# Fourier heads of a hybrid diffusion step: their map product moves into the last recurrent scan, their channel products beside the last recurrent norm, second half first

## The reference, cut to what matters

```python
o_h = o_f + jnp.flip(o_b, 1)
o_h = (_rms(o_h, hg_norm_w) * jax.nn.silu(hg.astype(F32).reshape(B, L, HG_HEADS, HG_DV)))
o_h = o_h.reshape(B, L, HG_WIDTH).astype(x.dtype)

xf = pft.astype(F32).reshape(B, L, FT_GROUPS, FT_CH)
mixed = jnp.real(jnp.fft.fft2(xf, axes=(1, 3), norm='ortho'))
o_ft = jnp.einsum('blgc,gce->blge', mixed, w_ft.astype(F32)).reshape(B, L, FT_WIDTH).astype(x.dtype)

mix = jnp.concatenate([o_attn, o_h, o_ft], axis=-1)
x = x + gate1 * jnp.einsum('blm,md->bld', mix, w_out)
```

## Time and profile before

| | us |
|---|---|
| median of 3 executions | 1788.07 |
| lowest, highest | 1786.11, 1788.44 |
| the profiled execution: its own time | 1787.74 |
| the profiled execution: span of the trace | 1785.9 |
| PE busy in the span | 1590.6 (89%) |
| DVE, ACT, POOL busy | 618.6, 387.3, 316.5 |
| mean granted TensorE clock | 0.944 of full speed |

### The profile page before, as it was taken

How to read it: one execution, slowest core, us unless ns; L and a number is a source line. 1 busy time by engine, 2 the same in 40 slices (tenths; PEclk the granted TensorE clock), 3 DMA queues, 4 the chain that set the end, 5 groups by cost and what they waited for, 6 DMA issues and landing times.

```text
span 1785.9 us, 24904 instructions
## 1 busy us (share of the span) xinstructions
PE 1590.6 (89%) x10358; PEld 1158.8 (65%) x10358; DVE 618.6 (35%) x1214; ACT 387.3 (22%) x718; POOL 316.5 (18%) x305
## 2 busy tenths in 40 slices
PE   6999989777898899999969998987879859999995
PEld 5556567556555788888755655766655458888883
DVE  1241246666115112222154312756631331221224
ACT  2231246222004100000142312632210210000002
POOL 4000159322000100000010001953300010000002
PEclk9999999878899899999979999998899969999997
DMA  9922100413022999999962211022400079999985
GB/s 267 327 54 69 50 27 2 143 52 94 0 71 107 340 363 366 365 363 359 339 237 47 67 52 50 2 72 73 120 1 1 1 272 329 369 371 365 370 303 212
DMA packets 143497, 315.69 MB, mean 177 GB/s; under 512 B 25025, under 2 KB 99193, under 8 KB 130457
## 3 DMA queue, kind: packets, MB, share of 16 engines
q1 hardware_dynamic: 120240, 241.88, 39.9%
q0 software_dynamic: 11104, 37.26, 5.4%
q10 hardware_dynamic: 12040, 34.95, 4.9%
HBM read 279.46 MB, written 34.60 MB: 176 GB/s over the span
## 4 chain that ended last, share of the span: by engine, by line
PE 77%; DVE 8%; ACT 4%; DMA 4%; POOL 3%; issue 3%; ACTq 0%; POOLq 0%; DVEq 0%
PE ps L1368 21%; PE ps L1771 20%; PE ps L1785 9%; PE ps L1412 4%; PE ps L1608 3%; ACT scr L576 3%; PE ps L1488 3%; POOL scr L507 3%; PE ps L1755 3%; PE ps L1668 2%; PE ps L1548 1%; DVE xT L1349 1%; DMA pT<-h_rows,slot_tok 1%; PE ps L1511 1%; PE ps L1631 1%
## 5 line engine op out<-in xcount | busy, mean ns | idle before, releaser
L1771 PEld LDWEIGHTS ps<-hT,ring 128*128 128x128 f32 x3200 | 370.3, 194 | 26.6 <-issue 22.0
L1771 PE MATMUL ps<-hT,ring 128*128 128x128 f32 x3200 | 371.1, 277 | 3.4 <-ACT hT L576 3.4
L1368 PE MATMUL ps<-hT,ring 128*128 128x512 f32 x960 | 266.9, 440 | 8.4 <-ACT hT L576 7.0
L1368 PEld LDWEIGHTS ps<-hT,ring 128*128 128x128 f32 x960 | 148.8, 194 | 129.0 <-issue 127.4
L576 ACT ACTIVATE pT<-ps 128x256 f32<-128x256 f32 (+3 forms) x74 | 33.4, 458 | 676.6 <-PE ps L1771 495.0
L1785 PE MATMUL ps<-ring,pT 128*128 128x512 f32 x400 | 179.6, 592 | 0.0
L548 POOL DMA_INDIRECT pT<-h_rows,slot_tok x50 | 47.2, 944 | 727.8 <-PE ps L1755 430.1
L1368 PE MATMUL ps<-pT,ring 128*128 128x512 f32 (+1 forms) x512 | 139.0, 434 | 1.7 <-ACT pT L576 1.7
L507 POOL TENSOR_SCALAR scr<-scr,st 128x640 f32<-128x640 f32 (+1 forms) x80 | 128.7, 1626 | 42.9 <-DVE st L1036 42.8
L1323 DVE TENSOR_TENSOR pT<-ps,pT 128x256 f32<-128x256 f32 x50 | 21.2, 425 | 328.6 <-ACT pT L576 328.6
L1785 PEld LDWEIGHTS ps<-ring,pT 128*128 128x128 f32 x400 | 72.3, 190 | 72.7 <-issue 72.7
(11 more groups left out here) (227 smaller groups left out, 1795.2 us busy)
## 6 DMA issues: line engine op xcount, KB each, us to landing
ring<-in_w_gate_dram SPq DMA_DIRECT2D x50, 1024.0 KB, 8.1
ring<-in_w_up_dram SPq DMA_DIRECT2D x50, 1024.0 KB, 8.0
ring<-in_w_down_dram SPq DMA_DIRECT2D x50, 1024.0 KB, 7.2
ring<-in_w_ada_dram SPq DMA_DIRECT2D x48, 1024.0 KB, 5.6
y_rows<-pT ACTq DMA_DIRECT2D x50, 512.0 KB, 8.5
ring<-in_w_in_dram SPq DMA_DIRECT2D x14, 1024.0 KB, 10.1
h_rows<-scr ACTq DMA_DIRECT2D x10, 512.0 KB, 2.6
ring<-in_w_in_dram SPq DMA_DIRECT2D x16, 256.0 KB, 4.5
```

What stands on the lines that cost most here:

```text
L1368: ins = mm(out[:, a:b], lhs, rhs[:, a:b], start=start, stop=stop, **kw)
L1771: last = mm(bank(2 + j, P, at + c * P), w[:, k, c * P:(c + 1) * P], xk[:, j, k, :], start=(k == 0), stop=(k == KC - 1))
```

## The change

PE's order. The map product moves from behind the norm to the last scan, (p, d) = (1, 1), between the last scores and L1639 (in the changed kernel L1645), and writes bank 2 instead of bank 6. The channel products move ahead of the wait for `on_ok`, right behind the norm's sum over channels; half 1 is first, and half 0, whose columns 0 to 1279 overlap the columns that ACT's Ln reads, waits for `on_rs`. The position DFT runs half 1 first, into banks 6 and 5, and half 0 into banks 3 and 4, without a wait for ACT in between. The output projection takes tile 13 (half 0) last of its 8 and waits for ACT's copies of the two halves only at the tiles that need them.

```diff
@@ ScalarE
-                for p in range(2):
-                    n = 2 * l + p
-                    act.wait_ge(f_o, n + 1)
-                    A_(pT[:, C_FT + p, NP:], bank(6), ACT.Copy).then_inc(f_os, 1)
-                    A_(pT[:, C_FT + p, 0:NP], bank(7, NP), ACT.Copy).then_inc(f_os, 1)
+                act.wait_ge(f_z, 2 * l + 1)
+                A_(scr_flat[:, 2560:3840], ps[:, 1536:2816], ACT.Copy).then_inc(f_za, 1)
+                for p in (1, 0):
+                    act.wait_ge(f_o, 2 * l + 2 - p)
+                    wide, narrow = (bank(6), bank(5, NP)) if p == 1 else (bank(3), bank(4, NP))
+                    A_(pT[:, C_FT + p, NP:], wide, ACT.Copy).then_inc(f_os, 1)
+                    A_(pT[:, C_FT + p, 0:NP], narrow, ACT.Copy).then_inc(f_os, 1)
@@ VectorE
                     n = 2 * l + p
+                    if p == 1:
+                        dve.wait_ge(f_ab, l + 1)
+                        V.tensor_copy(scr_flat[:, 3840:4352], bank(2)).then_inc(f_abs, 1)
                     dve.wait_ge(on_rs, n + 1)
...
+                dve.wait_ge(f_z, 2 * l + 2)
+                V.tensor_copy(scr_flat[:, 1280:2560], ps[:, 0:1280]).then_inc(f_zs, 1)
                 modulations(l, 1)
-                dve.wait_ge(f_ab, l + 1)
-                V.tensor_copy(scr_flat[:, 0:512], bank(6)).then_inc(f_abs, 1)
-                for p in range(2):
-                    n = 2 * l + p
-                    dve.wait_ge(f_z, n + 1)
-                    V.tensor_copy(scr_flat[:, 1280 * (1 + p):1280 * (2 + p)], ps[:, 1536 * p:1536 * p + 1280]).then_inc(f_zs, 1)
@@ TensorE
+                        if (p, d) == (1, 1):
+                            pe.wait_ge(g_used, g0 + 8)
+                            for a in range(4):
+                                last = mm(bank(2, P, a * P), K["dft64"][:, a % 2, :], wft[:, l, a // 2, :], start=True, stop=True)
+                            last.then_inc(f_ab, 1)
                         pe.wait_ge(g_used, g0 + 9)
...
-
+                pe.wait_ge(f_abs, l + 1)
+                for p in (1, 0):
+                    if p == 0:
+                        pe.wait_ge(on_rs, 2 * (l + 1))
+                    for t in range(TT):
+                        last = mm(ps[:, 1536 * p + 256 * t:1536 * p + 256 * t + 256], pT[:, C_FT + p, t * P:(t + 1) * P],
+                                  scr_flat[:, 3840 + 256 * p:4096 + 256 * p], start=True, stop=True)
+                    last.then_inc(f_z, 1)
                 pe.wait_ge(on_ok, 2 * (l + 1))
                 pe.wait_ge(dft_in, 16 * len(LATE_CONSTS))
-                for p in range(2):
-                    for s in range(2):
-                        last = mm(bank(6, P, (2 * p + s) * P), K["dft64"][:, s, :], wft[:, l, p, :], start=True, stop=True)
-                last.then_inc(f_ab, 1)
-                pe.wait_ge(f_abs, l + 1)
-                for p in range(2):
-                    for t in range(TT):
-                        last = mm(ps[:, 1536 * p + 256 * t:1536 * p + 256 * t + 256], pT[:, C_FT + p, t * P:(t + 1) * P],
-                                  scr_flat[:, 256 * p:256 * p + 256], start=True, stop=True)
-                    last.then_inc(f_z, 1)
-                for p in range(2):
-                    n = 2 * l + p
-                    pe.wait_ge(f_zs, n + 1)
-                    if p == 1:
-                        pe.wait_ge(f_os, 2 * n)
+                for p in (1, 0):
+                    pe.wait_ge(f_za if p == 1 else f_zs, l + 1)
+                    wide, narrow = (bank(6), bank(5, NP)) if p == 1 else (bank(3), bank(4, NP))
...
-                pe.wait_ge(f_os, 4 * (l + 1))
...
-                        for k in range(KC):
-                            last = columns(out, w[:, k, j * P:(j + 1) * P], pT[:, MIX[k], :], WIDE, k == 0, k == KC - 1)
+                        order = [k for k in range(KC) if MIX[k] != C_FT] + [MIX.index(C_FT)]
+                        for k in order:
+                            if c == 0 and MIX[k] in (C_FT, C_FT + 1):
+                                pe.wait_ge(f_os, 4 * l + (4 if MIX[k] == C_FT else 2))
+                            last = columns(out, w[:, k, j * P:(j + 1) * P], pT[:, MIX[k], :], WIDE, k == order[0], k == order[-1])
```

More of the change, by code:

```diff
@@ L325, in build_program @@
         state_out = sem("state_out")
-        f_ab = sem("f_ab"); f_abs = sem("f_abs"); f_z = sem("f_z"); f_zs = sem("f_zs"); f_o = sem("f_o"); f_os = sem("f_os")
+        f_ab = sem("f_ab"); f_abs = sem("f_abs"); f_z = sem("f_z"); f_zs = sem("f_zs"); f_za = sem("f_za"); f_o = sem("f_o"); f_os = sem("f_os")
         op_ps = sem("op_ps"); x_mid = sem("x_mid")
@@ L1667, in _ @@
                     for i, (t, s) in enumerate((t, s) for t in range(4) for s in range(2)):
-                        mm(bank(6), z[:, 1 + t, s, :], K["dft_s"][:, s, t, :], start=(i == 0), stop=(i == 7))
+                        mm(wide, z[:, 1 + t, s, :], K["dft_s"][:, s, t, :], start=(i == 0), stop=(i == 7))
                     for s in range(2):
-                        last = mm(bank(7, NP), z[:, 0, s, :], K["dft_p"][:, s, 0, :], start=(s == 0), stop=(s == 1))
+                        last = mm(narrow, z[:, 0, s, :], K["dft_p"][:, s, 0, :], start=(s == 0), stop=(s == 1))
```

## The result

The changed kernel took 1762.3 us (median of 4 executions, 1760.0 to 1765.4) against 1787.42 for the kernel before, which was timed beside it (4 executions, 1786.11 to 1788.44): ratio 0.9863, 95% interval 0.9844 to 0.9881, so 21 to 28 us faster. The forecast was 1768.5 with a range of 1764 to 1774. The profiled execution took 1764.48 us.

The account below looks back on a forecast made before the run. PE was taken to bound the kernel, 77% of the chain, with waits around layer 0's Fourier heads; one high-clock and one low-clock layer save 19.6 us (10.9 + 8.8 or 12.1 + 7.5), giving 1768.5 us, range 1764 to 1774.

Parts of the forecast that it names:

- The map under the merge: Map product in PE's 1.7 us wait for DVE's last merge: hidden at high clock, 0.1 to 0.4 us delay at low.
- The norm off the path, the channel products beside it: PE goes from the sum over channels straight into channel products; half 0's wait for `on_rs` costs nothing, by 0.3 us.
- ACT's copy: ACT's new 1280-column copy out of PSUM: 1.24 us, ready 0.4 to 0.9 us early under half 0, price 0.
- Two waits for ACT: Waits before half 0's position DFT and before the output projection: 1.1 us each gone per layer.
- The sum at the high clock: From sum over channels to output projection, at high clock: 12.1 us saved in layer 0, 10.9 in layer 1.
- one layer high and one low: Mixed clock levels from the second norm's sum over channels on: 19.6 us saved, chance 0.45.
- both high: Rival: both layers at high clock from the second norm's sum on, 23.0 us saved, 1765; chance 0.25.
- The price of a low layer: Low clock at first, sum over channels 2.5 us, channel products 6.5: saves 8.8 in layer 0, 7.5 in layer 1.
- both low: Rival: both layers at low clock at first, 16.3 us saved, 1771.8; chance 0.20.

Follow-up runs that it names:

- the filler: The kernel before with the map's 4 products run once more, unread, in PE's gap under the last merge: median 1786.85 us, ratio 0.9995.
- the map alone: The kernel before with only the map product and DVE's copy of it moved under the last merge: median 1778.84 us, ratio 0.9939.
- the three kernels that put one wait back: Changed kernel with channel products waiting for on_ok, 1772.94 us; one bank pair for both DFT halves, 1766.98; output projection waiting for all ACT's copies, 1766.27.
- without the map: The changed kernel without the map product and its copy, channel products taking a constant instead, run twice: medians 1766.47 and 1765.19 us.
- the last kernel: Beyond the changed kernel: map under scan (0, 1)'s merge, channel products moved into gaps around both norms: median 1751.87 us, ratio 0.9782.

## Why the prediction missed: right in its parts at the high clock, wrong in the clock's cases

Step by step, as the prediction put them:

- **The map under the merge**: right. It costs nothing there; the 0.60 us still idle before L1645 is what was left of the gap.
- **The norm off the path, the channel products beside it**: right, by 3.7 us of wait that comes back when they are put behind it. Half 0's wait for `on_rs` cost nothing: the 20 channel instructions run in one piece of 4.48 us.
- **ACT's copy**: 1.24 us by its slope, 1.24 measured, 0.7 us early.
- **Two waits for ACT**: 1.1 each; 1.2 and 1.0 when put back.
- **The sum at the high clock**: 12.1 and 10.9; measured 12.0 and 10.8.
- **The step that failed** is the choice between the cases: "one layer high and one low 0.45; both high 0.25". I took the level at the second norm as a draw that the filling would improve a little, and so the likeliest case was the mixed one, 19.6. With something under the last merge the sum over channels of the second norm was at 1.35 us in 16 of 16 norms (the two layers of the changed kernel three times, of the filler, of the map alone, and of the three kernels that put one wait back). With the gap empty it was at the low level in 4 of 8 (the kernel before twice, and without the map twice). That the level behind an empty gap differs between executions was right; that it still does behind the filled one was wrong. In the first norm, whose gap is empty in all of these, it was low in 16 of 24, and not evenly: 5 of 12 in layer 0 and 11 of 12 in layer 1. In the last kernel, which fills both gaps, it was high in 4 of 4. The prediction argued its odds from three low norms of four, two of which were first norms, whose gap the change leaves empty. This step is 3.4 (23.0 less 19.6) of the 6.2 us between forecast and median.
- **The price of a low layer** was too high as well. The sum gave 3.3 and 3.4 us for it, since it took 6.5 us for the channel products, their time from before, where they stood behind a wait of 3.43 us. Right behind a low sum over channels they took 5.4, and the low layer cost 2.0 us (22.14 against 20.13). With that the mixed case would have been 1767 and both low 1769.
- **The range and the rest.** The case of both layers high gives 1765, which lies inside the range; the other 2.8 us of the 6.2 took the median out of it. The range reached only 1 us past that case for the spread of executions. The changed kernel alone lay between 1760.0 and 1765.4 in its first four, and the kernel before between 1782.94 and 1794.39 in 23 of one batch. That the profiled execution came so near to the case, 1764.48, is in part luck: with the same two stretches the other two profiled executions took 1760.03 and 1763.07.

Two causes of the clock's level are to be kept apart, and the runs do so: the filling decides the level of the norm that follows it (the filler, and the kernels without the map), and the missing wait behind the sum decides the level of the channel products (the filler, the map alone, and the kernel with the products behind the norm all kept the sum at 1.35 and lost about 1.8 us or more in the products). The change needs both for its 20.13 us. The Trainium skill (TensorE: Matmul & The Clock Gate, Part 1, What's actually happening) says both that the gate goes by how busy the array has been and that the point of turning is tied to no place in the program. The empty gaps fit the second (3 of 4 low in layer 0, 1 of 4 in layer 1), and the filled ones fit the first (16 of 16 high).

**Open.** The stretches account for 22.8 us against the first profile of the kernel before and 23.9 against the second. All 12 executions of the changed kernel have a mean of 1763.0, the 47 of the kernel before that were timed beside it and the experiments one of 1788.9: 26.0 us, with two standard errors of 1.4. Outside the two stretches the profiles of the kernel before took 1722.9 and 1724.2 us, those of the changed kernel 1722.4, 1717.9 and 1720.9. With the experiments there are four profiles of the kernel before and its variants, with a mean of 1722.8, and eight of the changed kernel and its variants, from 1717.9 to 1726.1 with a mean of 1721.0. A difference of 1.8 us can't be told from chance there. Most of the spread lies between layer 0's output projection and layer 1's first norm, 764.3 to 772.6 us, where the change only reorders the projection's products and PE was busy 708.9 to 715.9 us with the same products. So some 2 us are saved elsewhere or are chance in how fast those products ran; no run here was made for it, and it stays open.

## What to carry to other kernels

Idle time of PE, the engine that bounds this kernel, was paid twice: once for itself, and once for the clock of what followed. Look in the timeline for short gaps of PE just before a dense stretch, and put independent products there; moving the map alone took 7.6 us out of the two stretches, where its own time and hand-offs had been 5.2. When a term depends on the clock's level, count how often the same place is low over several profiles before giving it a chance, and ask which of the gaps around it the change fills, not only whether it is low now. Price the low level by what will stand ahead of the products after the change, and not by their time from before. Take the range at least as wide as the executions of one kernel spread.

## What the runs showed of the hardware that was not expected

- With about 1.2 us of products in a gap of 1.7 the following sum over channels ran at the high level in all 16 cases, where it was low behind 4 of 8 empty gaps. Behind the wait of 3.4 or 3.5 us that followed such a sum of 1.35 us the clock was low again each time, 0.50 and 0.52 in the two windows above; the channel products took 6.24 us or more in all 8 of these stretches, against 4.48 without the wait.
- The spread of executions of one unchanged kernel was 11.5 us over 23, more than the whole effect of most single terms here; terms of 1 us were only readable in the traces, where at the high clock they repeated to 0.02 us.
